# A hybrid attention and mLSTM block on one core: in each attention step PE transposes this step's probabilities before it takes the next step's scores

## The reference, cut to what matters

```
def row_block(r):                      # neighbourhood attention, one row of 64 queries
    s_loc = einsum('bchd,bacwhd->bhcaw', q_r, k_win) + bias     # 8 x 16 local keys
    s_ctx = einsum('bchd,bnhd->bhcn', q_r, k_ctx)               # 256 context keys
    p = softmax(concatenate([s_loc, s_ctx]))
    return einsum(p_loc, v_win) + einsum(p_ctx, v_ctx)
...
att_c = softmax(qc @ kc) @ vc          # the context tokens attend to the context
y = depthwise_conv(glu, conv_w) + conv_b       # 31 taps, 512 features
out_lat = concatenate([att_lat, silu(layer_norm(y))]) @ w_out
```

## Time and profile before

| | |
|---|---|
| median of 3 runs | 1968.57 us (1965.87 to 1973.45) |
| the profiled execution's own time | 1973.65 us |
| its span, first to last instruction | 1971.8 us |
| PE busy | 1768.8 us (90%) |
| DVE busy | 844.2 us (43%) |
| ACT busy | 559.9 us (28%) |
| POOL busy | 276.9 us (14%) |
| mean granted clock of TensorE | 0.921 |

### The profile page before, as it was taken

How to read it: one execution, slowest core, us unless ns; L and a number is a source line. 1 busy time by engine, 2 the same in 40 slices (tenths; PEclk the granted TensorE clock), 3 DMA queues, 4 the chain that set the end, 5 groups by cost and what they waited for, 6 DMA issues and landing times.

```text
span 1971.8 us, 26385 instructions
## 1 busy us (share of the span) xinstructions
PE 1768.8 (90%) x10440; PEld 1459.5 (74%) x10440; DVE 844.2 (43%) x1217; ACT 559.9 (28%) x901; POOL 276.9 (14%) x204
## 2 busy tenths in 40 slices
PE   5989897588999999999999468988989989999997
PEld 4877675367888888888888467666757768787886
DVE  4377686634422222222223525556545443333333
ACT  3334454242321112211222302332333232122131
POOL 0396999500000000000000000000000000000000
PEclk8999898689999999999999759898869999999999
DMA  7623332022113421233215301001002323323333
GB/s 301 76 75 108 101 125 97 1 86 64 44 63 105 148 89 63 59 138 134 63 64 192 120 0 43 22 33 32 22 11 75 128 75 96 95 88 94 96 96 106
DMA packets 47314, 168.99 MB, mean 86 GB/s; under 512 B 5392, under 2 KB 5648, under 8 KB 47120
## 3 DMA queue, kind: packets, MB, share of 16 engines
q1 hardware_dynamic: 31408, 115.47, 18.4%
q10 hardware_dynamic: 15072, 51.53, 7.3%
q0 software_dynamic: 768, 1.08, 0.7%
HBM read 163.83 MB, written 4.19 MB: 85 GB/s over the span
## 4 chain that ended last, share of the span: by engine, by line
PE 78%; DVE 8%; POOL 6%; ACT 3%; issue 2%; DMA 2%; SPq 0%; ACTq 0%; DVEq 0%; POOLq 0%
PE PS L445 57%; PE PS L1643 5%; POOL X L392 3%; PE PS L1537 3%; POOL X L394 2%; PE PS L1546 2%; PE PS L1767 2%; PE PS L1869 2%; DMA scr<-in_ada 2%; PE PS L1868 1%; DVE scr L1416 1%; PE PS L1843 1%; PE PS L1597 1%; DVE w_lo L430 1%; DVE h_lo L963 1%
## 5 line engine op out<-in xcount | busy, mean ns | idle before, releaser
L445 PE MATMUL PS<-h_hi,w_hi 128*128 128x512 f32 (+1 forms) x1296 | 401.0, 364 | 3.7 <-DVE w_lo L430 3.2
L445 PE MATMUL PS<-h_lo,w_hi 128*128 128x512 f32 (+1 forms) x1296 | 394.0, 358 | 0.0
L445 PE MATMUL PS<-h_hi,w_lo 128*128 128x512 f32 (+1 forms) x1296 | 393.8, 358 | 0.0
L430 DVE TENSOR_TENSOR w_lo<-raw,w_hi 128x1024 fp32r<-128x1024 f32 x196 | 240.9, 1231 | 280.3 <-ACT w_hi L425 267.3
L425 ACT ACTIVATE w_hi<-raw 128x1024 fp32r<-128x1024 f32 x196 | 206.2, 1052 | 299.5 <-PE PS L445 244.1
L445 PEld LDWEIGHTS PS<-h_hi,w_hi 128*128 128x128 f32 x1296 | 217.7, 192 | 47.8 <-DVE w_lo L430 5.6
L445 PEld LDWEIGHTS PS<-h_lo,w_hi 128*128 128x128 f32 x1296 | 216.8, 191 | 37.1
L445 PEld LDWEIGHTS PS<-h_hi,w_lo 128*128 128x128 f32 x1296 | 215.5, 190 | 37.3
L445 PE MATMUL PS<-c_hi,w_hi 128*128 128x512 f32 (+1 forms) x688 | 215.9, 367 | 24.7 <-DVE c_lo L1009 18.7
L445 PE MATMUL PS<-c_lo,w_hi 128*128 128x512 f32 (+1 forms) x688 | 213.4, 363 | 0.0
L445 PE MATMUL PS<-c_hi,w_lo 128*128 128x512 f32 (+1 forms) x688 | 212.4, 362 | 0.0
(11 more groups left out here) (259 smaller groups left out, 2055.6 us busy)
## 6 DMA issues: line engine op xcount, KB each, us to landing
raw<-in_w SPq DMA_DIRECT2D x196, 512.0 KB, 3.4
scr<-in_ada ACTq DMA_DIRECT2D x48, 512.0 KB, 5.7
adaw<-in_ada ACTq DMA_DIRECT2D x32, 512.0 KB, 4.3
scr<-in_ada SPq DMA_DIRECT2D x8, 1024.0 KB, 10.6
X<-in_xT SPq DMA_DIRECT2D x4, 768.0 KB, 6.8
X<-in_xT ACTq DMA_DIRECT2D x1, 3072.0 KB, 9.9
x_spill<-X ACTq DMA_DIRECT2D x1, 2048.0 KB, 9.3
X<-x_spill ACTq DMA_DIRECT2D x1, 2048.0 KB, 8.6
```

Source lines behind the costliest of these rows:

```text
L430: nc.vector.tensor_tensor(w_lo[:, j], raw[:, j].rearrange("p (k n) -> p k n", k=KT), w_hi[:, j].bitcast(f32), ALU.subtract).then_inc(s_lo, 1)
L445: last = nc.tensor.matmul(G[j][:, a:b], w[:, j, k], m[:, k, a:b], start=(n == 1), stop=(n == 3 * k_tiles))
```

## The change

Two lines of PE's list change places in the loop over the attention steps. In step U, `transpose_probs(U)` is issued before `scores(U + 1)`. No instruction is added or removed, every wait stays with its instruction, and the lists of DVE, ACT, POOL and SP are the same.

```diff
             scores(0)
             for U in range(NU):
+                transpose_probs(U)
                 if U + 1 < NU:
                     scores(U + 1)
-                transpose_probs(U)
```

## The result

The changed kernel takes 1988.76 us (median of 7 runs, 1985.45 to 1991.49). The kernel before, run beside it, takes 1973.45 us (7 runs, 1965.87 to 1978.67). The ratio is 1.0085, 95% interval 1.0069 to 1.0101, so +16.8 us (13.6 to 19.9): slower, and clear of the 0.5% that the prediction took as what a measurement can tell. (Microseconds are the ratio times 1973; the two medians differ by 15.3.) The prediction was 1983.3, range 1973 to 1993. The profiled execution took 1991.28 us, its span is 1989.5.

The account below looks back on a forecast made before the run. POOL and the round of PE, DVE and ACT were taken to bound the attention in alternating stretches; 4.3 + 2.0 + 3.1 + 5.3 = 14.7 us took the median from 1968.57 to 1983.3, range 1973 to 1993.

Parts of the forecast that it names:

- First merge, +4.3: Steps 0 to 2: scores start behind the transposes, so DVE's first merge comes 4.3 us later (bounds 2.0 and 5.3).
- Steps 6 and 7, +2.0: Up to the second merge: nothing covers the two blocks of transposes, +2.0 us (bounds 0 and 3.1).
- at random in each step: All steps: moved DVE work meets other POOL instructions, returning a microsecond more or less; the sum would stay.
- Steps 8 to 12, +0: Up to the third merge: five blocks of 0.95, 4.8 us, lie in DVE's 9.7 us wait, adding nothing.
- Steps 13 to 18, +3.1: Third to fourth merge: late masks and DVE's own way exceed its wait, +3.1 us (bounds 0 and 6.7).
- Tail, +5.3: Steps 19 to 23, after POOL is done: scores behind transposes delay the maxima, +5.3 us (bounds 2.5 and 9.3).
- Hidden: Rival: DVE's waits of 9.7 and 8.0 us swallow more, steps 0 to 2 pay little; 6.5 us, 1975, chance 0.18.
- The slow clock: Rival: new PE waits of 2 to 4 us bring half clock in every late step; 9 us more, 1992, chance 0.12.
- the sign of being wrong (less than 3): The prediction called itself wrong if the second merge came less than 3 us late.
- DVE's wait of 8.0: DVE's wait for POOL at the fourth merge: forecast all but gone; 4 us or more left would mean hidden.

Follow-up runs that it names:

- the repeat: The changed kernel timed and profiled once more as it is, against the kernel before (6 runs): ratio 1.0098 [1.0081, 1.0115], +19.3 us.
- with filling: Changed kernel plus matrix products nobody reads, put into PE's waits in some steps; against the kernel before 1.0042 [1.0022, 1.0061], +8.3 us.
- the free bank: Changed kernel with attention outputs of steps 17 to 21 in PSUM bank 3, so transposes don't wait for attn_lo; against the kernel before 1.0082, +16.2 us.
- the scores between the two half blocks: All steps: transposes of head 1, then next scores, then transposes of head 0; against the kernel before 1.0028 [1.0013, 1.0042], +5.5 us.

## Why the prediction was right, and where it was off

**The kind and the size.** The step that carried the prediction was right: nothing is gained by earlier transposes, and ready scores stand behind ones that come first in PE's list. DVE's waits for scores grew from 14.6 to 40.7 us. The forecast of +14.7 us stands beside +16.8 (13.6 to 19.9) and, in the repeat, +19.3 (16.0 to 22.7), inside the first interval and below the second, so it is at the low end. Of the 5.5 us between 1983.3 and 1988.76, 4.9 are that the kernel before has a median of 1973.45 over seven runs, where three gave 1968.57; the profiled execution, 5.1 above that median, was the better base. Of the terms, three held and two were mis-sized, against each other. That the total came so close is in part luck: the profiled attention is +21.9 (+17.7 in the repeat), and in the first of the two profiles 2.9 us of it went again behind the attention.

**First merge, +4.3.** Held: +4.1 with these steps alone, +4.3 in the repeat. In the first profile it is +6.4. The 2.2 us more lie behind attend(1), where PE went to half clock after a wait of 1.76 us: from attend(1) to the merge it is 19.4 us, and 16.3 with these steps alone and in the repeat.

**Steps 6 and 7, +2.0.** Mis-sized. The maximum of step 8, counted from that of step 6, is late by 2.2 with these steps alone, as written, and by 1.1 in the changed kernel (1.5 in the repeat), but DVE's next operations meet less of POOL and give 0.8 to 1.5 back. Alone the two steps add 0.7 to the stretch, in the changed kernel 0.5 (0.9 in the repeat), and by the times nothing. The prediction named such a gain as one that comes "at random in each step"; here it was a shift that let DVE fall between POOL's instructions. The Trainium skill (SBUF — State Buffer, "Who interferes with whom") has the one that comes second wait for the whole instruction, and the rows of this pair agree: L1166 took 0.97 us in one and 0.43 in the other, and the longer one ended at 238.19, just behind POOL's addition (L394, 236.56 to 238.16).

**Steps 8 to 12, +0.** Held by the times (+1.0, interval -2.0 to +3.9), though the profiles have 0.5 to 1.8 us more in the third stretch; of that 1.2 is also there in two profiles that leave these steps alone (65.7 us).

**Steps 13 to 18, +3.1.** This is the term that was off most: +7.5. It had two parts. The maximum of step 15 was to be 3.6 us later against the third merge. It is 7.4 later in the changed kernel and its repeat (21.0 for 13.6), which both were at half clock from attend(13) or just behind it; it is 4.3 later with these steps alone, with filling and with the free bank, all three at full clock there. So some 3.1 of the excess go with that stretch of half clock, and 0.7 with the queue. The second part was that DVE's way from there loses 7.4 and has 8.0 to lose, -0.6. DVE lost all 8.0 and 0.1 more: from the maximum of 15 to the merge it is 50.7 us for 50.6, with a wait of 8.0 in the one and none in the other. As the prediction had it, both ways to the fourth merge came out equally long: POOL's last tap, late by its masks, ended at 386.98, and DVE, without waiting, began the merge at 387.19.

**Tail, +5.3.** +6.3, +4.5 in the repeat and +6.2 with these steps alone, by the profiles; held. The timed ratio of those steps alone, +10.1 with at least 6.5, is more than that, and it isn't known where; one tail of 34.3 us in the order before shows that the base of 36.7 can be 2 us long.

**The rivals.** Hidden (+6.5) is excluded by the total, whose interval begins at 13.6, and by DVE's wait at the fourth merge, which is gone. The slow clock was given 0.12, with 9 us more than the forecast, on the ground that rows bear it out "not for those of 2 to 3 us". That ground was too thin: it rested on one row, attend(7) after 1.73 us at full clock. In this case waits of 1.76, 1.93 and 2.95 us were followed by half clock, others of 1.76 and 2.32 us by full clock. Filled products took 9.3 us back, but the forecast's sum had counted half clock in about half of the late steps already. The measured excess over it is 2 to 5 us, and the rival's total, 9 above the forecast (+23.7), lies above both intervals. The Trainium skill (TensorE: Matmul & The Clock Gate, "HAM oscillation — how this bites in real kernels") describes an engine that idles between bursts and starts each at half clock; the rows behind attend(13) agree in the changed kernel and its repeat (L1546 in 1.93 us), and those of attend(1) agree in one execution and not in the other.

**What was to be seen.** Merges were forecast at 186, 250.5, 315 and 382; they came at 186.7, 249.8, 315.4 and 387.2, and in the repeat at 185.6, 249.0, 314.0 and 385.8. The third is close because this execution began its attention 1.3 us early: up to there the stretches add up to +8.1, where 6.3 was written. The second merge is 5.6 us late, so the sign of being wrong (less than 3) didn't come. DVE's wait of 8.0 is gone, and the first output projection is 20.6 us later, not 14 to 15 (17.3 in the repeat). DVE waits for PE before each maximum of steps 16 to 23, by 1.7 to 3.2 us, as written.

## What to carry to other kernels

In an engine's list, an instruction that has all it needs should stand ahead of one that waits, above all where the ready one feeds the longer way round; look for the work and the wait that it would inherit. Here it was, by elimination, mostly the work: with the scores between the two half blocks, 11.3 of 16.8 us came back, while taking away the wait for the shared bank gave nothing that the times show. Count such a move stretch by stretch between the waits of the other engines: where another engine waits longer than the delay, it is free, and elsewhere the stretches add. Where the moved order opens new pauses in TensorE like those here (1.76 to 2.95 us), price the products behind them at half clock as one case and try a few unread products in the pause.

## What the runs showed of the hardware

A short wait does not set the clock by its length alone. After the same 1.76 us ahead of attend(1), with the same list, the changed kernel ran at half clock in one execution (granted 0.54 from 168 to 175 us) and at full clock in another:

```profile
168.00:175.00 7.00, 7.00 (x58) 5.73 (x54) 2.26 (x4) 2.93 (x6) 0.00 (x0) 0.54 0.45 152
```

The repeat, where attend(1) starts at 169.29:

```profile
168.00:175.00 7.00, 5.71 (x69) 4.93 (x70) 4.14 (x8) 4.83 (x9) 0.00 (x0) 1.00 0.35 122
```

In nine of the fourteen profiles attend(7) waits 1.70 to 1.76 us; in four of them the small products behind it ran at full clock (L1546 in 1.08 us) and in five at half clock (up to 1.94 us). Both occur where the order up to there is unchanged, and both in the changed kernel. Such a stretch of half clock cost 3.1 us behind attend(1), where the round is the bound; behind attend(7) DVE's wait for POOL took up the 3.8 to 5.3 us that it cost the round, all but 1.2 at most.

The scatter is larger than one would think from a median of three. The kernel before ran from 1965.5 to 1983.9 us over 35 executions in one set of rounds, and the part behind the attention, which no kernel here changed, took 1559 to 1571 us in the profiles. An effect of 2 us or less, such as that of steps 6 and 7, can't be read from a dozen runs. It can be read from landmarks in the trace, if the same landmarks of other profiles show how far they scatter.
